# Two queues for the first loads, finer slices of them, and a new order of the first roundings

## What is computed

```python
def short_conv_mixer(h, w_in, conv_w, w_out):
    bcx = h @ w_in
    b_gate, c_gate, xv = jnp.split(bcx, 3, axis=-1)
    u = b_gate * xv
    ...
def first_block(x, ...):
    for i in range(DEPTH):
        h = rmsnorm(x, norm_mixer[i])
        mix = short_conv_mixer(h, ...) if i % 2 == 0 else swa_sink_attention(h, ...)
        x = x + mix
        x = x + swiglu_ffn(rmsnorm(x, norm_ffn[i]), ...)
    return x
```

## Time and profile before

| | us |
|---|---|
| median of 3 runs | 1021.85 |
| lowest, highest | 1021.8, 1023.05 |
| the profiled execution | 1021.8 |
| its span, first to last instruction | 1020.0 |
| TensorE busy in it | 1002.8 |
| start of the first useful matmul | 9.92 |
| start of body 1 on TensorE | 23.13 |

### The profile page before, as it was taken

The page is one execution under the profiler, slowest core; times in us unless marked ns, Lnnn a source line. Parts: engine busy times, 40 slices in busy tenths (PEclk is TensorE's granted clock), DMA queues, the critical chain, the costliest instruction groups (busy, mean ns, idle before and its releaser), DMA issues.

```text
span 1020.0 us, 19467 instructions
## 1 busy us (share of the span) xinstructions
PE 1002.8 (98%) x6598; PEld 908.2 (89%) x6598; DVE 724.1 (71%) x1122; ACT 616.7 (60%) x1108; POOL 264.1 (26%) x249
## 2 busy tenths in 40 slices
PE   8999999999999999999999999999999999999998
PEld 6899888889998788888898999899999988888886
DVE  5997788786667668777766687577866868774443
ACT  6556666664556767666654567857474568764332
POOL 2441223221212322222212136402031435441000
PEclk9999999999999999999999999999999999999999
DMA  8674555545552225545545555444444535455531
GB/s 317 221 309 173 181 196 200 186 174 187 197 186 104 84 89 203 203 171 199 184 162 205 192 173 196 171 165 165 140 157 164 195 132 207 170 199 189 183 124 42
DMA packets 35534, 180.90 MB, mean 177 GB/s; under 512 B 3344, under 2 KB 5520, under 8 KB 17680
## 3 DMA queue, kind: packets, MB, share of 16 engines
q1 hardware_dynamic: 35472, 180.07, 50.1%
HBM read 179.01 MB, written 1.05 MB: 177 GB/s over the span
## 4 chain that ended last, share of the span: by engine, by line
PE 93%; ACT 2%; DVE 2%; issue 1%; POOL 1%; DMA 1%; SPq 0%; POOLq 0%; ACTq 0%; DVEq 0%
PE bank L458 30%; PE bank L464 26%; PE bank L460 11%; PE bank L462 11%; PE bank L502 4%; PE bank L501 4%; PE bank L500 4%; PE bank L645 1%; DMA raw<-in_stream 1%; ACT pr L1051 1%; PE bank L635 1%; DVE wlo L1308 0%; POOL pr L1852 0%; PE bank L817 0%; PE bank L710 0%
## 5 line engine op out<-in xcount | busy, mean ns | idle before, releaser
L1308 DVE TENSOR_TENSOR wlo<-raw,whi 128x1024 fp32r<-128x1024 f32 (+1 forms) x296 | 364.2, 1231 | 92.4 <-ACT whi L850 89.8
L850 ACT ACTIVATE whi<-raw 128x1024 fp32r<-128x1024 f32 (+2 forms) x296 | 308.8, 1044 | 124.6 <-PE bank L464 117.2
L464 PE MATMUL bank<-xa,wlo 128*128 128x256 f32 x1696 | 354.6, 280 | 0.0
L458 PE MATMUL bank<-xa,whi 128*128 128x512 f32 x1088 | 348.4, 397 | 3.7 <-DVE wlo L1308 2.4
L464 PEld LDWEIGHTS bank<-xa,wlo 128*128 128x128 f32 x1696 | 302.6, 189 | 42.7
L458 PEld LDWEIGHTS bank<-xa,whi 128*128 128x128 f32 x1088 | 170.2, 189 | 11.5 <-DVE wlo L1308 3.1
L460 PE MATMUL bank<-xa,whi 128*128 128x256 f32 x608 | 165.0, 290 | 0.1
L462 PE MATMUL bank<-xa,whi 128*128 128x256 f32 x608 | 160.9, 283 | 0.0
L875 ACT ACTIVATE spill<-bank 128x256 f32<-128x256 f32 x152 | 58.1, 382 | 129.1 <-PE bank L464 129.1
L460 PEld LDWEIGHTS bank<-xa,whi 128*128 128x128 f32 x608 | 116.4, 191 | 2.5 <-issue 1.9
L462 PEld LDWEIGHTS bank<-xa,whi 128*128 128x128 f32 x608 | 116.5, 192 | 0.3
(11 more groups left out here) (225 smaller groups left out, 1388.8 us busy)
## 6 DMA issues: line engine op xcount, KB each, us to landing
raw<-in_stream SPq DMA_DIRECT2D x138, 1024.0 KB, 4.8
raw<-in_stream SPq DMA_DIRECT2D x44, 512.0 KB, 5.1
raw<-in_stream SPq DMA_DIRECT2D x8, 768.0 KB, 4.2
bias<-in_bias SPq DMA_DIRECT2D x1, 3072.0 KB, 12.9
x<-in_x SPq DMA_DIRECT2D x2, 512.0 KB, 5.9
out<-x SPq DMA_DIRECT2D x3, 256.0 KB, 2.4
cons<-in_cons SPq DMA_DIRECT2D x1, 640.0 KB, 9.1
out<-x SPq DMA_DIRECT2D x2, 128.0 KB, 2.4
```

The costliest lines, as they stand in the source:

```text
L458: pe.matmul(dst, whi[:, slot, at + i, :], X[:, k, :, :], start=first and i == 0, stop=False)
L464: ins = pe.matmul(narrow, wlo[:, slot, at + i, :], X[:, k, 0, :], start=False, stop=last and i == len(tiles) - 1)
L850: act.activation(whi[:, p, 0:kts, :].rearrange("p k m -> p (k m)"), src, ACT.Copy)\
L1308: dve.tensor_tensor(wlo[:, p, 0:kts, :].rearrange("p k m -> p (k m)"), src, whi[:, p, 0:kts, :].rearrange("p k m -> p (k m)").bitcast(F32) ...
```

## The change

Loads. x comes in four transfers of two tiles instead of two of four, and they are issued by ScalarE, with `vecs` behind the first. SyncE issues weights only: piece 0 in two halves of four k-tiles, then pieces 1, 2 and 3, then `cons` and `sinks` as before. Each of these has a semaphore of its own or shares one that isn't waited for in between.

So this rounding no longer stands behind the wait for the norm. The diff, cut:

```diff
-WARMING = 9
+WARMING = 5
...
-            sp.dma_start(vecs[:], vecs_in).then_inc(vecs_loaded, 16)
-            sp.dma_start(x[:, 0:4, :], x_in[:, 0:4, :]).then_inc(x_loaded[0], 16)
...
+            for i in range(2):
+                dst, src = first_chunk(0)
+                half = slice(i * PIECE // 2, (i + 1) * PIECE // 2)
+                sp.dma_start(dst[:, half], src[:, half]).then_inc(first_half[i], 16)
+            for p, loaded in ((1, raw_loaded[0]), (2, third_raw), (3, raw_loaded[1])):
+                dst, src = first_chunk(p)
+                sp.dma_start(dst, src).then_inc(loaded, 16)
...
-            AS_LOADED = [(0, 4, 0), (0, 4, 1), (4, 8, 0), (4, 8, 1), (0, 8, 2), "norm", (0, 8, 3)]
+            AS_LOADED = [(0, 4, 0), (4, 8, 0), (0, 8, 1), (0, 8, 2), "norm", (0, 8, 3)]
...
+            for i in range(4):
+                act.dma_start(x[:, 2 * i:2 * i + 2, :], x_in[:, 2 * i:2 * i + 2, :]).then_inc(x_loaded[i], 16)
+                if i == 0:
+                    act.dma_start(vecs[:], vecs_in).then_inc(vecs_loaded, 16)
             act.preload_act_table_set(LOGS)
...
             round_weights(0, 1, free=False)
-            act.wait_ge(x_loaded[1], 16)
-            first_tiles(range(4, 8))
             first_squares(range(2, 4))
-            act.wait_ge(first_raw[1], 16)
+            act.wait_ge(third_raw, 16)
             round_weights(0, 2, free=False)
-            first_squares(range(4, 6))
+            first_squares(range(4, 5))
             act.wait_ge(raw_loaded[1], 16)
             round_weights(0, 3, free=False)
-            first_squares(range(6, 8))
+            first_squares(range(5, 8))
...
                 spill_tile(4 * (B0["bx"] + i) + p, p)
+                round_weights(B0["bx"] + i + 1, p)
                 if i == 0 and p == 0:
                     rms(0)
-                round_weights(B0["bx"] + i + 1, p)
```

More of the change, by code:

```diff
@@ L205, in build @@
         vecs_loaded = sem("vecs_loaded")
-        x_loaded = [sem("x_loaded0"), sem("x_loaded1")]
-        first_raw = [sem("first_raw0"), sem("first_raw1")]
+        x_loaded = [sem(f"x_loaded{i}") for i in range(4)]
+        first_half = [sem("first_half0"), sem("first_half1")]
+        third_raw = sem("third_raw")
+        half_hi = sem("half_hi")
+        half_lo = sem("half_lo")
         raw_loaded = [sem("raw_loaded0"), sem("raw_loaded1")]
@@ L373, in _, with first_chunk @@
         def _(sp):
-            sp.dma_start(vecs[:], vecs_in).then_inc(vecs_loaded, 16)
-            sp.dma_start(x[:, 0:4, :], x_in[:, 0:4, :]).then_inc(x_loaded[0], 16)
-            for p in range(4):
+            def first_chunk(p):
                 at = chunk_offset(p // 2)
@@ L380, in _ @@
                 half = slice(p % 2 * PIECE, (p % 2 + 1) * PIECE)
[L381 to L384, removed]
+                return raw[:, p // 2, half], src[:, half]
+            for i in range(2):
[5 more added lines that the diff above has]
+                sp.dma_start(dst, src).then_inc(loaded, 16)
             def load(b, h, offset, size, waits):
@@ L911, in first_squares, with first_half_weights @@
                     square(t, 0, x[:, t, :])
+            def first_half_weights(i):
+                act.wait_ge(first_half[i], 16)
+                act.activation(whi[:, 0, 4 * i:4 * i + 4, :].rearrange("p k m -> p (k m)"),
+                               raw[:, 0, i * PIECE // 2:(i + 1) * PIECE // 2], ACT.Copy)\
+                   .then_inc(half_hi if i == 0 else hi_ready, 1)
             act.wait_ge(x_loaded[0], 16)
-            first_tiles(range(0, 4))
-            act.wait_ge(first_raw[0], 16)
-            round_weights(0, 0, free=False)
+            first_tiles(range(0, 2))
+            first_half_weights(0)
+            act.wait_ge(x_loaded[1], 16)
+            first_tiles(range(2, 4))
             first_squares(range(0, 2))
+            first_half_weights(1)
+            act.wait_ge(x_loaded[2], 16)
+            first_tiles(range(4, 6))
+            act.wait_ge(x_loaded[3], 16)
+            first_tiles(range(6, 8))
             act.wait_ge(raw_loaded[0], 16)
             round_weights(0, 1, free=False)
-            act.wait_ge(x_loaded[1], 16)
-            first_tiles(range(4, 8))
             first_squares(range(2, 4))
-            act.wait_ge(first_raw[1], 16)
+            act.wait_ge(third_raw, 16)
             round_weights(0, 2, free=False)
-            first_squares(range(4, 6))
+            first_squares(range(4, 5))
             act.wait_ge(raw_loaded[1], 16)
             round_weights(0, 3, free=False)
-            first_squares(range(6, 8))
+            first_squares(range(5, 8))
             def decay_constant(q):
@@ L1363, in _, with first_rest @@
                                      op0=ALU.mult, op1=ALU.mult).then_inc(kgain_ready, 1)
+            def first_rest(i):
+                if i == 0:
+                    dve.wait_ge(half_hi, 1)
+                else:
+                    dve.wait_ge(hi_ready, 1)
+                dve.tensor_tensor(wlo[:, 0, 4 * i:4 * i + 4, :].rearrange("p k m -> p (k m)"),
+                                  raw[:, 0, i * PIECE // 2:(i + 1) * PIECE // 2],
+                                  whi[:, 0, 4 * i:4 * i + 4, :].rearrange("p k m -> p (k m)").bitcast(F32), ALU.subtract)\
+                   .then_inc(half_lo if i == 0 else lo_ready, 1)
             for t in range(KT):
-                if t % 4 == 0:
-                    dve.wait_ge(x_loaded[t // 4], 16)
+                if t % 2 == 0:
+                    dve.wait_ge(x_loaded[t // 2], 16)
                 norm_lo(t, "mix0", SPLIT["mix0"])
-                if t == 3:
-                    rest_weights(0, 0, free=False)
-                    rest_weights(0, 1, free=False)
+                if t in (1, 3):
+                    first_rest(t // 2)
+            rest_weights(0, 1, free=False)
             rest_weights(0, 2, free=False)
```

7 lines of the change are left out of this document (5 added, 2 removed).

## The result

The changed kernel takes 1027.28 us (median of 6 runs, 1026.43 to 1028.05) against 1021.83 of before: a ratio of 1.005 with a 95% interval of 1.0039 to 1.006, half a per cent slower. The forecast was 1022.5, 0.7 us more than before, with a range of 1020.3 to 1024.9: the sign was right, the size wasn't, and the time lies 2.4 us above the range. The profiled execution took 1026.6 us with a span of 1024.8; it is the second shortest of the six, so the profiles differ by 4.8 us and the medians by 5.45.

A forecast was written before the change was run, and what follows sets the result against it. TensorE, busy for 1002.8 of 1020.0 us, was taken to bound the kernel. L = 11.0 put piece 1 at 14.3 and body 1 at 23.85 instead of 23.13, +0.7 on 1021.8: 1022.5 us, range 1020.3 to 1024.9.

The forecast's parts named there:

- What bounds, and the rest of body 0: TensorE sets the time; the change lies ahead of body 1's start at 23.13 us, with 996.9 us behind it unchanged.
- t + 9.53: Body 1's earliest start, where t is piece 1's start on TensorE: 16 x 0.355 + 0.67 + 3.18 us later.
- The swap: Body 1's first rounding moved ahead of the norm on ScalarE: the 0.39 us idle ahead of body 1 goes.
- The norm's sum: Five GpSimd additions in body 0, 5.87 us, ready at t + 5.0 and due at t + 5.68.
- What makes t: Piece 1's start on TensorE comes 3.3 us after x's fourth transfer lands, if ScalarE is free then.
- When things land: Landings of the first loads: x's fourth quarter between 10.3 us (sharing by bytes) and 11.7 us (order of issue).
- L: Landing of x's fourth transfer, taken as 11.0 us, which put piece 1's start at 14.3 us.
- rival 2: Queues alternate row by row: x's fourth quarter lands at 13.0 us, body 1 at 25.8, +2.7 us, 1024.5; chance 0.18.
- Rival 1: Early transfers overlap better, 420 GB/s: body 1 at 21.2 to 22.2 us, -1.9 to -0.9 us; chance 0.25.
- rival 3: TensorE falls back to 1.2 GHz: seven slow pairs from piece 1 on, +2.4 on top of +0.7, 1024.9; chance 0.14.
- The issues on ScalarE: Five issues at 0.46 us with the gap, ahead of ScalarE's 1.28 us table load, end at 4.3 us, hidden.
- The fourth piece: Its rounding ahead of three squares in body 0: ready at t + 3.8, due at t + 6.35, in time without the move.

The follow-up runs named there:

- hold: The changed kernel with one wait added: SyncE issues piece 2 and all behind it only when x's third quarter has landed; 1023.14 us, 1.0014 of before.
- fillers: The changed kernel with WARMING 9 and eight more matmuls on zeros in TensorE's pauses of body 0; 1026.2 us, 1.0042 of before.
- one_queue_warm5: The changed kernel with x and the constants back on SyncE's queue, all of x ahead of pieces 1 to 3, WARMING still 5; 1021.78 us.
- one_queue: The changed kernel with x and the constants back on SyncE's queue, ahead of pieces 1 to 3, and WARMING 9; 1022.5 us, 1.0004 of before.
- warm9: The changed kernel with WARMING 9 instead of 5; 1027.37 us, 1.005 of before.
- queues_only: The kernel before with both halves of x and the constants between them on ScalarE's queue; 1026.3 us, 1.0038 of before.
- swap_warm12: The kernel before with body 1's first rounding ahead of the norm and WARMING 12; 1021.38 us, 0.9994 of before.

## Why the prediction was wrong

- **What bounds, and the rest of body 0 (right, in part by luck).** All of the difference lies ahead of body 1, and t + 9.53 held wherever the pace did: 9.56 in hold, 9.57 in fillers, 9.58 in one_queue_warm5. But the terms were off and made up for each other: the 16 pairs and the norm took 5.80 and 0.75 in hold instead of 5.68 and 0.67, and the last piece 3.01 instead of 3.18. The swap removed the idle time as worked out, and 0.18 us more. The norm's sum, for which the text had a margin of 0.7, had none: the additions took 6.6 us instead of 5.9 and ended at 19.61 in hold, 0.14 ahead of the norm's first matmul.
- **What makes t (right).** From the start of x's last tiles to piece 1 it was 16.64 - 13.47 = 3.17, forecast 3.2 to 3.3, and the first useful matmul came at 8.01 for 7.9.
- **When things land (wrong, the step that failed).** I put L between sharing by bytes, 10.3, and the order of issue, 11.7, took the middle, and left turns by rows as a rival of 0.18. The landing was 13.4: 2.4 us behind L = 11.0, and even behind that rival's 13.0. The reason given for the bounds, that one queue in its order of issue is all that the trace shows, is no ground for leaving out a third way of sharing. The packets of the trace were rows already, and a count of rows, 640 of x and constants beside 640 of weights, sets x's end at the 3149 KB that rival 2 had. Its 13.0 rests on a "mean step" of 1.4 that leaves out the first step, 2.1; all four steps, 6.3 us, give 1.6 each and a landing at 13.3. Rival 1's 4.4 to 5.4 for 589 KB has a slip too: at 420 GB/s and a trail of 1.0 to 1.4 it is 4.4 to 4.8.
- **The rivals, taken one at a time (wrong).** Rival 2 gave +2.7 and rival 3 +2.4, and I priced "alone or with the others" with the end of one of them. I argue that they aren't independent: a later x means longer pauses of TensorE. The single profiles go that way only in part (2.06 us lost to the pace at t = 16.64 and 1.83 at 17.38, 0.33 at 15.54, none at 13.95, but 1.39 at 14.17 in one_queue). Their sum, +5.1 us, is what body 1's start shows. That it fits to 0.1 is luck: the parts were +3.04 for 2.7 and +2.06 for 2.4. A range to 1026.9 would have followed from the numbers in the text; the median lies 0.4 above even that.
- **The pace (mechanism half right).** The short warming did leave TensorE at the slower pace at first: the pairs at 8.8 and 9.5 us are 0.64 and 0.72 apart, rival 3's sign. That cost nothing, since TensorE waited anyway, and by 12.80 the faster pace was there. What cost 2.06 us was a fall at 14.7, and that isn't the short warming's: with nine matmuls it fell as well (warm9), and with five and one queue it didn't in body 0. It fell behind a stretch that was busy for 1.03 of 3.50 us, and with matmuls in the pauses it didn't fall in the profiled execution (fillers).
- **The issues on ScalarE (right).** Four took 0.40 to 0.45 each and the last 0.57, the table load began at 3.22 and nothing waited for it.
- **The fourth piece (right).** No gain by itself.

## What to carry to other kernels

Where the DMA engines are busy a second queue adds little: the changed kernel moved 3.31 MB in its first 12 us, the same slices on one queue 3.02, and the kernel before, with longer rows on one queue, 3.32. What it changes is who goes first, and it does so by rows, so that a transfer with short rows beside one with long rows gets less than half. Keep what is needed in one order on one queue, or hold the later loads back by a wait, which alone gave 4.1 us of 5.45 here. And where two rivals have one cause, price them together, as one case.

## What the runs showed of the hardware

- Turns by rows: 729 packets with 2.21 MB beside 698 with 1.10 MB in the same 12 us. The Trainium skill, "DMA: Bandwidth & Descriptors", section "Rules for kernel authors", says that spreading loads over issuing engines doesn't help and only saves the time of issue. Here it did harm, +4.5 us in queues_only, by changing the order in which the bytes came.
- 77 KB of constants took 7.2 us from issue behind 512 KB of x on ScalarE's queue, with two pieces beside them (queues_only), and 4.6 in the changed kernel behind a 256 KB quarter, with two halves beside them; on one queue, issued first, 1.9 to 2.0.
- The granted clock fell to 0.50 behind stretches in which TensorE was busy for 1.03 of 3.50 us (changed kernel, longest pause 1.78), 1.53 of 3.20 (one_queue, 1.92) and, at 355 us, 1.48 of 3.00 (swap_warm12). It cost 1.4 to 2.1 us where dense work followed at once, and 1.0 to 1.3 at 355 us. But in one_queue_warm5 TensorE was busy for 3.69 of 6.40 us ahead of t and kept its pace, and the kernel before was busy for 2.09 of 4.00 us from 352 us on and kept it too. When it falls isn't settled by these runs.
- The view of the clock reads 1.00 from 0 to 11.2 us of the changed kernel, where pairs are 0.64 apart, the pace of 1.2 GHz; the same holds for the warming of before. So a reading of 1.00 at the start doesn't show the faster pace, and the distance of the matmuls has to be read instead:

```profile
8.82 0.63 PE L463 MATMUL bank<-xa,whi 128*128 128x512 f32 x1
...
9.46 0.71 PE L463 MATMUL bank<-xa,whi 128*128 128x512 f32 x1
```
